# A two-block model kernel on one core: x loaded first and squared along rows, a stage's first block behind the evictions two blocks back, the residual ahead of the last modulation sum

## The chip, the cores and the metric

The kernel runs on one core of one Trainium2 chip. The core has TensorE (PE), VectorE (DVE), ScalarE (ACT), GpSimd (POOL), the sync engine (SP) that issues transfers, and 16 DMA engines that all queues share. The metric is the device time of one execution in microseconds (us). Lower is better.

## What is computed

The reference runs 512 tokens of width 1024 through two model blocks. The first has a gated linear recurrence (hgrn2), a sparse attention (nsa) and two swiglu layers, all with norms that are scaled and shifted by a modulation computed from a vector `c`. The second has a differential attention, a state-space layer (s5) and two squared-relu layers.

```
mods = einsum('bd,lde->lbe', silu(c), ada_w) + ada_b        # 4 x (1024 x 3072) products with one vector
shift, scale, gate = split(mods[2 * layer], 3)
h = rms_norm(x, gain) * (1 + scale) + shift                 # rms_norm: x * rsqrt(mean(x*x) + eps) * gain
x = x + gate * mixer(h)
... swiglu, then the second layer, then the second block
```

## The kernel before

Activations are kept transposed: `xT` is 128 partitions x 8 k-tiles x 512 tokens. Every weight product is done in blocks. A block is one weight tile of up to 128x2048 (1 MB), loaded into `raw` (a ring of two), split by ACT into a rounded part `whi` (`convert_hi`, L385) and by DVE into the rest `wlo` (`convert_lo`, L389), and multiplied by PE with the two parts `hh` and `hl` of the activations: three 512-column matmuls per 128x128 weight tile (L448, or L442 where the output is token-major; L426 and L430 in a stage that starts while its activations are still being made). PSUM has eight banks; a block with parity `par` writes banks `2 * par` and `2 * par + 1`, and banks 4 to 7 serve the sums.

The stages ("segments") stand in one list: h_q, h_f, h_v, h_g, h_out, ffn0_in0, ffn0_out0, ffn0_in1, ffn0_out1, n_kvc, n_ks, n_vs, n_kw, n_vw, n_q, n_out, then the same four ffn1 stages, d_q, d_k, d_v, d_out, the four mlp0 stages, s_glu and the four mlp1 stages. Each has `act` and `dve`, the number of its PSUM evictions per block that ACT and DVE do. The order of work on each engine is the order of the program; waits are on semaphores (`ev_a` and `ev_v` count evictions, `mm` counts finished units of PE, `w_lo` counts converted blocks). Before a block, `weight_products` waits for the evictions of the block two back, which used the same banks, counted by this stage's own rate. At a stage whose `(act, dve)` differs from the stage before, and that has no `need` of its own, `boundary` (L569) waits for all evictions of all stages before. There are nine such stages: h_v, ffn0_in1, n_vs, n_kw, n_vw, ffn1_in1, d_v, mlp0_in1 and mlp1_in1.

The start. SP issues the eight loads of `ada_first` (1 MB each, 128 rows of 8 KB, the first modulation matrix; a ring of six slots, so that the seventh and eighth load wait for `ada0_sum_v` and `ada0_used`, which say that DVE and PE have used a slot), then the weight loads `raw`. ACT issues five small constant loads, among them `ident` and `ones`, and then `xin` (x, 2 MB, rows of 4 KB). PE transposes the constants (L2582, waits for all five), multiplies the last four column groups of the first two modulation matrices with `cact` (L544), then transposes x into banks 0 to 3, 4 matmuls per k-tile (L2589). ACT squares each k-tile from PSUM into `sq` (L2160) and copies it to `xT` (L2161), and PE adds the squares over the partitions with a matmul by `ones` (L535, `first_square_sum`, 512 columns per k-tile) before it transposes on. Behind them stand the other six L544 groups and 12 matmuls (24 instructions) of `ada_sum` by `ones` (L556), which end the first modulation. DVE meanwhile multiplies and adds the eight `ada_first` tiles into `ada_sum` (L524, L527), then adds the bias (L2381), forms the gain (L2373), converts the first `wlo` and begins `apply`: for each k-tile xn = xT * gain * rstd (L2402), ACT makes `hh` (L2185), DVE makes `hl` (L2394). PE's first weight product is L426.

Later modulations are computed beside the stages: ACT loads (`ada_load`), DVE forms sums over k (`ada_sums`, L506 and L510, 8 instructions per block), PE adds them over the partitions (`ada_products`, L470) one block later, `ada_bias` adds the bias. In a stage that ends in a norm (`norm_after`: h_out, ffn0_out1, n_out and so on) DVE adds the residual (`residual`, L2439 or L2437), ACT squares it (L2202), PE sums the squares (`square_sums`, L2605), and at the end ACT makes `rstd` (L2177, L2178). Of these stages h_out alone also has modulation sums. In h_out's DVE code `ada_sums` stands ahead of the residual in every block, and in its PE code the last `ada_products` ahead of the last `square_sums`.

## Time and profile before

| | |
|---|---|
| median of 3 runs | 3031.37 us (3028.98 to 3031.47) |
| profiled execution | 3029.0 us |
| its span | 3027.3 us |
| PE busy | 2827.0 us, 93% of the span |
| DVE busy | 1654.6 us, 55% |
| ACT busy | 1063.9 us, 35% |
| mean granted TensorE clock | 0.968 |

The span is the time between the first and the last instruction that the profiler saw; the execution's own time is 1.7 us more. In a timeline row the columns are start in us, duration in us, engine, line, operation, output and inputs by the program's names, their sizes, and how many instructions were merged into the row; in brackets stands how long the engine had nothing to run before it and whose result ended that. Matmuls overlap, so a row's duration is longer than the distance to the next. ACTq and SPq rows are the issues of transfers, not their duration.

### The profile page before, as it was taken

The page shows a single profiled execution, that of the slowest core. Times are in us where ns is not written, and L with a number is a line of the kernel's source. Part 1 is how long each engine was busy: PE and PEld are TensorE (multiplying, and loading weights), DVE is VectorE, ACT ScalarE, POOL GpSimd, SP SyncE. Part 2 cuts the span into 40 slices and gives each one's busy share as a digit, 9 for nine tenths or more (in the row PEclk, how much of TensorE's full clock was granted, in tenths as well). Part 3 has the DMA queues.
Part 4 walks back from the last instruction along what each step waited for, and adds up shares of the span by engine and source line. Part 5 has one row for each costly group of instructions (what it writes and reads, how often), then busy time and mean ns, then how long its engine had stood idle before and what let it go on. Part 6 is the DMA issues. An engine that isn't in the chain of part 4 may idle for free.

```text
span 3027.3 us, 38551 instructions
## 1 busy us (share of the span) xinstructions
PE 2827.0 (93%) x14850; PEld 2262.7 (75%) x14850; DVE 1654.6 (55%) x2383; ACT 1063.9 (35%) x1577; POOL 75.2 (2%) x87
## 2 busy tenths in 40 slices
PE   6999999999988799999999998999999977999999
PEld 4898778888776556688787785777887756778787
DVE  4576566766453667433334557467677395353342
ACT  3312233222322367332223438433232534342231
POOL 2013000000000000000000100000000000000000
PEclk9999999999999799999999999999999988999999
DMA  5640356564424000232333330143444671223332
GB/s 212 195 140 1 112 153 191 163 182 144 154 86 128 1 1 1 56 83 81 107 84 111 114 100 13 42 100 103 141 153 153 230 125 57 84 83 98 97 97 70
DMA packets 400811, 321.14 MB, mean 106 GB/s; under 512 B 14409, under 2 KB 387233, under 8 KB 399649
## 3 DMA queue, kind: packets, MB, share of 16 engines
q1 hardware_dynamic: 324096, 237.19, 26.7%
q10 hardware_dynamic: 74496, 77.77, 7.9%
q0 software_dynamic: 2080, 4.26, 0.6%
q8 instruction: 96, 1.57, 0.2%
q14 instruction: 43, 0.34, 0.0%
HBM read 293.05 MB, written 19.86 MB: 103 GB/s over the span
## 4 chain that ended last, share of the span: by engine, by line
PE 64%; issue 22%; DVE 8%; ACT 2%; DMA 2%; POOL 1%; SPq 0%; ACTq 0%; DVEq 0%; POOLq 0%
PE ps L448 45%; PE ps L426 4%; PE ps L442 2%; PE ps L430 2%; DVE ada_acc L1749 1%; PE ps L873 1%; PE ps L903 1%; PE ps L885 1%; PE ps L1617 1%; PE ps L2605 1%; DVE h_area L1751 1%; DVE h_area L1753 1%; DMA xin<-in_x 1%; PE ps L1658 1%; POOL kT L1829 1%
## 5 line engine op out<-in xcount | busy, mean ns | idle before, releaser
L448 PE MATMUL ps<-hh,whi 128*128 128x512 f32 x1744 | 690.8, 396 | 5.1 <-DVE xT L2439 1.6
L448 PE MATMUL ps<-hh,wlo 128*128 128x512 f32 x1744 | 680.7, 390 | 0.0
L448 PE MATMUL ps<-hl,whi 128*128 128x512 f32 x1744 | 680.1, 390 | 0.0
L389 DVE TENSOR_TENSOR wlo<-raw,whi 128x2048 fp32r<-128x2048 f32 x198 | 453.9, 2292 | 359.7 <-ACT whi L385 359.7
L385 ACT ACTIVATE whi<-raw 128x2048 fp32r<-128x2048 f32 x198 | 377.3, 1906 | 380.8 <-PE ps L448 257.7
L448 PEld LDWEIGHTS ps<-hh,whi 128*128 128x128 f32 x1744 | 328.1, 188 | 79.3 <-issue 11.8
L448 PEld LDWEIGHTS ps<-hl,whi 128*128 128x128 f32 x1744 | 328.2, 188 | 70.3 <-issue 3.8
L448 PEld LDWEIGHTS ps<-hh,wlo 128*128 128x128 f32 x1744 | 327.9, 188 | 69.2
L448 PE MATMUL ps<-hid_h,whi 128*128 128x512 f32 x756 | 307.4, 407 | 0.0
L448 PE MATMUL ps<-hid_l,whi 128*128 128x512 f32 x756 | 298.9, 395 | 0.0
L448 PE MATMUL ps<-hid_h,wlo 128*128 128x512 f32 x756 | 298.8, 395 | 0.0
L448 PEld LDWEIGHTS ps<-hid_h,whi 128*128 128x128 f32 x756 | 142.2, 188 | 37.5 <-issue 4.3
L448 PEld LDWEIGHTS ps<-hid_l,whi 128*128 128x128 f32 x756 | 142.2, 188 | 37.4 <-issue 4.3
L448 PEld LDWEIGHTS ps<-hid_h,wlo 128*128 128x128 f32 x756 | 142.0, 188 | 34.6
L510 DVE SCALAR_TENSOR_TENSOR ada_ring<-ada_ring,cact 128x256 f32<-128x256 f32 (+1 forms) x336 | 151.8, 452 | 12.1
L2202 ACT ACTIVATE sq<-xT 128x512 f32 (+1 forms) x56 | 35.3, 632 | 291.5 <-DVE xT L2439 138.8
L2437 DVE TENSOR_TENSOR xT<-xT,ps 128x512 f32 (+1 forms) x40 | 27.4, 686 | 165.8 <-PE ps L448 144.7
L2263 ACT ACTIVATE hid_h<-hid_f 128x512 f32 (+1 forms) x44 | 27.8, 632 | 246.6 <-DVE hid_f L2485 246.6
L426 PE MATMUL ps<-hh,whi 128*128 128x512 f32 x176 | 78.0, 443 | 38.4 <-ACT hh L2185 38.4
L2325 ACT ACTIVATE act_t<-ps 128x512 f32<-128x512 f32 x64 | 38.0, 597 | 194.8 <-PE ps L448 185.9
L2539 DVE TENSOR_TENSOR hid_f<-act_t 128x512 f32<-128x512 f32 x64 | 43.4, 688 | 103.7 <-ACT act_t L2325 103.3
L2485 DVE TENSOR_TENSOR hid_f<-act_t,ps 128x512 f32<-128x512 f32 x44 | 30.2, 687 | 126.3 <-PE ps L448 121.3
(401 smaller groups left out, 4130.8 us busy)
## 6 DMA issues: line engine op xcount, KB each, us to landing
raw<-in_ffn_w_in SPq DMA_DIRECT2D x44, 1024.0 KB, 6.0
ada_ring<-in_ada_w ACTq DMA_DIRECT2D x82, 512.0 KB, 4.4
raw<-in_ffn_w_up SPq DMA_DIRECT2D x32, 1024.0 KB, 5.4
raw<-in_ffn_w_down SPq DMA_DIRECT2D x32, 1024.0 KB, 5.8
raw<-in_ffn_w_out SPq DMA_DIRECT2D x32, 704.0 KB, 4.6
raw<-in_hgrn_w_in SPq DMA_DIRECT2D x16, 1024.0 KB, 5.8
raw<-in_attn_w_qkv SPq DMA_DIRECT2D x12, 1024.0 KB, 5.1
s_area<-cp_dram SPq DMA_DIRECT2D x6, 2048.0 KB, 9.8
```

The source lines that it names most:

```text
L385: nc.scalar.activation(whi[:, par, :], raw[:, par, :], ACT.Copy).then_inc(w_hi, 1)
L389: nc.vector.tensor_tensor(wlo[:, par, :], raw[:, par, :], whi[:, par, :].bitcast(F32), ALU.subtract).then_inc(w_lo, 1)
L426: nc.tensor.matmul(ps[:, 2 * par + j, :], tile(w, kt, j), hi[:, kt, :], start=(kt == 0 and n == 0), stop=False)
L430: m = nc.tensor.matmul(ps[:, 2 * par + j, :], tile(wh, kt, j), lo[:, kt, :], start=False, stop=(kt == k - 1))
L442: m = nc.tensor.matmul(ps[:, bank, half * 256:half * 256 + 256], x[:, kt, t0:t0 + P], w[:, kt, :], start=(kt == 0 and n == 0), stop=(kt == ...
L448: m = nc.tensor.matmul(ps[:, bank, :], tile(w, kt, j), x[:, kt, :], start=(kt == 0 and n == 0), stop=(kt == k - 1 and n == 2))
L510: nc.vector.scalar_tensor_tensor(out=acc if last else w[:, 0, :], in0=w[:, kt, :], scalar=cact[:, kt:kt + 1], in1=w[:, 0, :], op0=ALU.mult ...
L873: m = nc.tensor.matmul(ps[:, S_BANK[w % 2] + i, 0:n], nqr[rows, p, t * P:(t + 1) * P], (k_sel, k_win)[br][rows, p // 2, 0:n], start=False, ...
L885: m = nc.tensor.transpose(ps[:, 2 + i, kt * P:(kt + 1) * P], pbuf[:, 2 * (w % P_SLOTS) + i, kt * P:(kt + 1) * P], ident[:, :])
L2202: nc.scalar.activation(sq[:, q:q + 1, :], xT[:, bass.ds(b * s.dve + j, 1), :], ACT.Square).then_inc(sq_rdy, 1)
L2325: nc.scalar.activation(act_t[:, j, :], ps[:, 2 * par + j, :], ACT.Relu).then_inc(ev_a, 1)
L2539: nc.vector.tensor_tensor(hid_f[:, j, :], act_t[:, j, :], act_t[:, j, :], ALU.mult).then_inc(hidf_rdy, 1)
```

## The change

The diff does three things.

1. The start. SP issues the load of x ahead of `ada_first`; ACT no longer issues it. PE transposes x right behind the constants, with the first L544 group (k-tile 0 of the modulation) after the fourth k-tile of x and the second after the eighth. ACT copies each k-tile of x to `xT`, and after every second one squares one 128-token tile of `xin` along its row (128x1024) with an accumulated output `x_ssq`, one column per tile. DVE, between its fourth and fifth modulation sum, spreads each column on a diagonal (`ident * x_ssq`, 128x128, four times), and PE multiplies these by `ones` (four matmuls of 128 columns in place of eight of 512). The 12 `ada_sum` matmuls run the scale columns (8 to 11) first, in bank 4, then the shift columns (0 to 7), in bank 6, and signal each part. DVE forms scale and gain after the first part, makes the first two xn, and only then waits for the second part, adds the shift and converts the first `wlo`.
2. Boundaries. Where `(act, dve)` changes and the stage has no `need`, the first block now waits as the stages with a `need` do, for the evictions up to the block two back, and `boundary` stands ahead of the second block.
3. h_out's last block. DVE does the residual first and `ada_sums` behind it; PE does the last `square_sums` ahead of the last `ada_products`.

```diff
--- before.py
+++ after.py
@@ -233,7 +233,7 @@
         ev_a = sem("ev_a")
         ev_v = sem("ev_v")
         const_a, const_in = sem("const_a_in"), sem("const_in")
-        x_in = sem("x_in")
+        x_in, x_sq = sem("x_in"), sem("x_squares")
         sq_rdy, ssq_rdy, rstd_rdy = sem("sq_rdy"), sem("ssq_rdy"), sem("rstd_rdy")
         xn_rdy, hh_rdy, hl_rdy = sem("xn_rdy"), sem("hh_rdy"), sem("hl_rdy")
         a_link, v_link, pool_set = sem("a_link"), sem("v_link"), sem("pool_set")
@@ -526,14 +526,26 @@
                     dve.wait_ge(ada0_sum_v, kt)
                     nc.vector.scalar_tensor_tensor(out=ada_sum[:, :], in0=w, scalar=c, in1=ada_sum[:, :],
                                                    op0=ALU.mult, op1=ALU.add).then_inc(ada0_sum_v, 1)
+                if kt == 3:
+                    first_square_spread(dve)
             dve.wait_ge(cols_ps, 2)
             link(nc.vector.tensor_copy(cols_b[:, 0:NROW_B], ps[:, 5, 0:NROW_B]))

-        def first_square_sum(pe, kt):
-
-            pe.wait_ge(sq_rdy, kt + 1)
-            nc.tensor.matmul(ps[:, 7, :], ones[:, :], sq[:, kt % 2, :], start=(kt == 0),
-                             stop=(kt == KT - 1)).then_inc(ssq_rdy, 1)
+        x_ssq = gains_a[:, 4, 0:TT]
+
+        def first_square_spread(dve):
+
+            for t in range(TT):
+                dve.wait_ge(x_sq, t + 1)
+                nc.vector.tensor_scalar(rstd[:, t * P:(t + 1) * P], ident[:, :], x_ssq[:, t:t + 1], None, ALU.mult
+                                        ).then_inc(sq_rdy, 2)
+
+        def first_square_sums(pe):
+
+            for t in range(TT):
+                pe.wait_ge(sq_rdy, 2 * t + 2)
+                nc.tensor.matmul(ps[:, 7, t * P:(t + 1) * P], ones[:, :], rstd[:, t * P:(t + 1) * P], start=True, stop=True,
+                                 skip_group_check=True).then_inc(ssq_rdy, 2)

         def ada_first_pe(pe, k0, k1):

@@ -552,10 +564,11 @@
             if k1 < FIRST:
                 return
             pe.wait_ge(ada0_sum_v, FIRST)
-            for j in range(NV):
-                m = nc.tensor.matmul(ps[:, 4, j:j + 1], ada_sum[:, j * P:j * P + P], ones[:, 0:1],
-                                     start=False, stop=True, skip_group_check=True)
-            m.then_inc(ada0_used, 1)
+            for bank, part in ((4, range(KT, NV)), (6, range(KT))):
+                for j in part:
+                    m = nc.tensor.matmul(ps[:, bank, j:j + 1], ada_sum[:, j * P:j * P + P], ones[:, 0:1],
+                                         start=(j == 0), stop=True, skip_group_check=True)
+                m.then_inc(ada0_used, 1)

         def ada_bias(dve, s):

@@ -2053,6 +2066,7 @@
         @block.sync
         def _(sp):

+            sp.dma_start(xin[:, :, :], a["x"][0].rearrange("(t p) d -> p t d", p=P)).then_inc(x_in, 16)
             for kt in range(FIRST):
                 if kt >= 6:
                     sp.wait_ge(ada0_sum_v, kt - 5)
@@ -2149,16 +2163,19 @@
             act.dma_start(vec_a[0:96, :], a["ada_b"].rearrange("l (c n) -> (l c) n", n=P)).then_inc(const_a, 16)
             act.dma_start(vec_a[96:112, :], a["kv_ada_b"].rearrange("(c n) -> c n", n=P)).then_inc(const_a, 16)
             act.dma_start(ones[:, :], a["k_ones"]).then_inc(const_a, 16)
-            act.dma_start(xin[:, :, :], a["x"][0].rearrange("(t p) d -> p t d", p=P)).then_inc(x_in, 16)
             act.wait_ge(cols_rdy, 1)
             nc.scalar.activation(cact[:, :], cols_a[:, ROWS["c"]:ROWS["c"] + 8], ACT.Silu).then_inc(cact_rdy, 1)
             log_table()
+            act.wait_ge(x_in, 16)
             for kt in range(KT):
                 act.wait_ge(mm, kt + 1)
-                if kt >= 2:
-                    act.wait_ge(ssq_rdy, kt - 1)
-                nc.scalar.activation(sq[:, kt % 2, :], ps[:, kt % 4, :], ACT.Square).then_inc(sq_rdy, 1)
                 nc.scalar.activation(xT[:, kt, :], ps[:, kt % 4, :], ACT.Copy).then_inc(ev_v, 1)
+                if kt % 2:
+                    t = kt // 2
+                    if t >= 2:
+                        act.wait_ge(x_sq, t - 1)
+                    nc.scalar.activation((sq, xn)[t % 2][:, :, :].rearrange("p s n -> p (s n)"), xin[:, t, :], ACT.Square,
+                                         accum_out=x_ssq[:, t:t + 1]).then_inc(x_sq, 1)
             act.wait_ge(pool_set, 2)

             def norm(m, x_count):
@@ -2378,9 +2395,12 @@
             ada_first_dve(dve, link)
             dve.wait_ge(ada0_used, FIRST + 1)
             dve.wait_ge(cols_rdy, 1)
-            link(nc.vector.tensor_tensor(mods[:, 0:16], ps[:, 4, 0:16], cols_a[:, 0:16], ALU.add))
-            modulated_gain(0, ROWS["norm_mix"], 8).then_inc(mods_rdy, 1)
-            if upto >= 2:
+            link(nc.vector.tensor_tensor(mods[:, 8:16], ps[:, 4, 8:16], cols_a[:, 8:16], ALU.add))
+            link(modulated_gain(0, ROWS["norm_mix"], 8))
+
+            def first_shift():
+                dve.wait_ge(ada0_used, FIRST + 2)
+                nc.vector.tensor_tensor(mods[:, 0:8], ps[:, 6, 0:8], cols_a[:, 0:8], ALU.add).then_inc(mods_rdy, 1)
                 convert_lo(dve, segs[0], 0, 0, 0)

             def apply(j, m, gain, shift, h_free):
@@ -2402,14 +2422,20 @@
                     nc.vector.scalar_tensor_tensor(out=xn[:, k % 2, :], in0=xT[:, kt, :],
                                                    scalar=gain[:, kt:kt + 1], in1=rstd[:, :],
                                                    op0=ALU.mult, op1=ALU.mult).then_inc(xn_rdy, 1)
+                    if j == 0 and kt == 1:
+                        first_shift()
                     if kt:
                         low(k - 1)
                 low(KT * j + KT - 1)

             def linear(s, evac):
                 def body(b, par, more):
-                    ada_sums(dve, s, b, par)
+                    late = s.name in norm_after and isinstance(b, int) and b == s.n - 1
+                    if not late:
+                        ada_sums(dve, s, b, par)
                     evac(b, par)
+                    if late:
+                        ada_sums(dve, s, b, par)
                     if s.name in D0:
                         d_hook_dve(dve, link, D0[s.name] + b)
                     if more:
@@ -2451,7 +2477,6 @@
                 return evac

             if upto >= 2:
-                dve.wait_ge(mods_rdy, 1)
                 apply(0, 0, *mod_cols(0), FIRST_UNITS)
                 convert_lo(dve, segs[0], 0, 1, 1)
                 linear(seg["h_q"], none)
@@ -2580,18 +2605,18 @@
         def _(pe):
             pe.wait_ge(const_a, 16 * 5)
             nc.tensor.transpose(ps[:, 6, 0:NROW_A], vec_a[0:NROW_A, :], ident[0:NROW_A, 0:NROW_A]).then_inc(cols_ps, 1)
-            ada_first_pe(pe, 0, 2)
             pe.wait_ge(x_in, 16)
             for kt in range(KT):
                 if kt >= 4:
                     pe.wait_ge(ev_v, kt - 3)
                 for t in range(TT):
-                    m = nc.tensor.transpose(ps[:, kt % 4, t * P:(t + 1) * P], xin[:, t, kt * P:(kt + 1) * P],
-                                            ident[:, :])
+                    m = nc.tensor.transpose(ps[:, kt % 4, t * P:(t + 1) * P],
+                                            xin[:, t, kt * P:(kt + 1) * P], ident[:, :])
                 m.then_inc(mm, 1)
-                if kt:
-                    first_square_sum(pe, kt - 1)
-            first_square_sum(pe, KT - 1)
+                if kt % 4 == 3:
+                    ada_first_pe(pe, kt // 4, kt // 4 + 1)
+            ada_first_pe(pe, 2, 4)
+            first_square_sums(pe)

             def square_sums(s, m, b, par):

@@ -2618,9 +2643,7 @@

                 prev = segs[segs.index(s) - 1] if s.g0 else None
                 change = prev is not None and (prev.act, prev.dve) != (s.act, s.dve)
-                if change and need is None:
-                    boundary(pe, s)
-                elif change:
+                if change:
                     if s.ea0 - prev.act > 0:
                         pe.wait_ge(ev_a, s.ea0 - prev.act)
                     pe.wait_ge(ev_v, s.ev0 - prev.dve)
@@ -2630,7 +2653,7 @@

                 def body(b, par, more):
                     first = isinstance(b, int) and b == 0
-                    if change and need is not None and isinstance(b, int) and b == 1:
+                    if change and isinstance(b, int) and b == 1:
                         boundary(pe, s)
                     weight_products(pe, s, b, par, hi, lo, token_major, need if first else None)
                     if s.ada and not first:
@@ -2644,12 +2667,12 @@
                     unrolled(s, body, D0, lambda db: d_hook_pe(pe, db))
                 else:
                     each_block(pe, s, body, need is not None or m is not None or s.ada is not None)
-                ada_products(pe, s, s.n - 1, (s.g0 + s.n - 1) % 2)
                 if m is not None:
                     square_sums(s, m, s.n - 1, (s.g0 + s.n - 1) % 2)
+                ada_products(pe, s, s.n - 1, (s.g0 + s.n - 1) % 2)

             if upto >= 2:
-                ada_first_pe(pe, 2, FIRST)
+                ada_first_pe(pe, 4, FIRST)
                 linear(seg["h_q"], need=(hl_rdy, 0))
                 linear(seg["h_f"])
                 linear(seg["h_v"], token_major=True)
```

## Rows read from the trace of the kernel before

**Rows 1.** The page's first part: busy time, share of the span, instructions.
```profile
PE 2827.0 (93%) x14850; PEld 2262.7 (75%) x14850; DVE 1654.6 (55%) x2383; ACT 1063.9 (35%) x1577; POOL 75.2 (2%) x87
```

**Rows 2.** Timeline, issues of the first transfers on the ACT and SP queues.
```profile
0.82 19.15 SPq L2060 DMA_DIRECT2D ada_first<-in_ada_w  x8
...
3.54 0.56 ACTq L2152 DMA_DIRECT2D xin<-in_x  x1
...
20.02 102.32 SPq L2075 DMA_DIRECT2D raw<-in_hgrn_w_in  x9
```

**Rows 3.** Stretches: length, busy PE PEld DVE ACT POOL; clock, DMA share, GB/s.
```profile
24.00:28.00 4.00, 0.00 (x0) 0.00 (x0) 3.79 (x3) 0.00 (x0) 0.00 (x0) 1.00 1.01 417
...
47.50:53.00 5.50, 5.21 (x25) 5.12 (x25) 0.17 (x1) 0.00 (x0) 0.00 (x0) 0.50 0.00 0
```

**Rows 4.** Timeline of PE from 14 to 58 us.
```profile
14.92 0.46 PE L2582 MATMUL ps<-ident,vec_a 120*128 120x120 f32 x1 [14.92 <-DMA ones<-in_k_ones]
...
29.29 1.97 PE L2589 MATMUL ps<-ident,xin 128*128 128x128 f32 x8 [9.72 <-DMA xin<-in_x]
...
43.83 3.76 PE L544 MATMUL ps<-cact,ada_first 128*128 128x1 f32 x32
47.45 5.26 PE L556 MATMUL ps<-ones,ada_sum 128*128 128x1 f32 x24
57.00 0.77 PE L426 MATMUL ps<-hh,whi 128*128 128x512 f32 x1 [4.29 <-ACT hh L2185]
```

**Rows 5.** Timeline of DVE up to 57 us.
```profile
29.71 1.82 DVE L527 SCALAR_TENSOR_TENSOR ada_sum<-ada_first,cact,ada_sum 128x1536 f32<-128x1536 f32 x1 [1.18 <-DMA ada_first<-in_ada_w]
...
52.80 0.17 DVE L2381 TENSOR_TENSOR mods<-ps,cols_a 128x16 f32<-128x16 f32 x1 [8.49 <-PE ps L556]
...
55.30 1.41 DVE L2402 SCALAR_TENSOR_TENSOR xn<-xT,gains_a,rstd 128x512 f32<-128x512 f32 x2
```

**Rows 6.** Timeline of ACT up to 46 us.
```profile
15.96 1.28 ACT L642 ACT_TABLE_LOAD   x1
...
30.93 0.59 ACT L2161 ACTIVATE xT<-ps 128x512 f32<-128x512 f32 x1
...
43.50 1.89 ACT L385 ACTIVATE whi<-raw 128x2048 fp32r<-128x2048 f32 x1
```

**Rows 7.** Timeline of PE where a stage's first block waits at a boundary.
```profile
151.37 0.39 PE L442 MATMUL ps<-whi,hh 128*128 128x256 f32 x1 [0.49 <-ACT kT L2222]
...
610.01 0.47 PE L448 MATMUL ps<-hh,whi 128*128 128x512 f32 x1 [0.70 <-issue]
...
846.56 0.39 PE L442 MATMUL ps<-whi,hh 128*128 128x256 f32 x1 [0.69 <-ACT nsa_area L2222]
...
859.16 0.47 PE L448 MATMUL ps<-hh,whi 128*128 128x512 f32 x1 [0.83 <-issue]
...
1464.72 0.39 PE L448 MATMUL ps<-hid_l,whi 128*128 128x512 f32 x1
1464.96 0.40 PE L448 MATMUL ps<-hid_h,wlo 128*128 128x512 f32 x1
1466.90 0.47 PE L448 MATMUL ps<-hh,whi 128*128 128x512 f32 x1 [1.55 <-DVE xT L2439]
...
2840.59 0.49 PE L448 MATMUL ps<-hh,whi 128*128 128x512 f32 x1 [1.32 <-DVE xT L2437]
```

**Rows 8.** Timeline of DVE, last block of h_out and the norm behind it.
```profile
406.44 0.35 DVE L506 TENSOR_SCALAR ada_ring<-ada_ring,cact 128x256 f32<-128x256 f32 x1 [0.82 <-DMA ada_ring<-in_kv_ada_w]
...
410.42 1.40 DVE L2439 SCALAR_TENSOR_TENSOR xT<-ps,mods,xT 128x512 f32<-128x512 f32 x2
414.50 2.29 DVE L389 TENSOR_TENSOR wlo<-raw,whi 128x2048 fp32r<-128x2048 f32 x1 [2.68 <-ACT whi L385]
...
416.98 1.42 DVE L2402 SCALAR_TENSOR_TENSOR xn<-xT,gains_a,rstd 128x512 f32<-128x512 f32 x2
```

**Rows 9.** Timeline of PE beside it, behind h_out's last weight product.
```profile
408.84 1.96 PE L2605 MATMUL ps<-sq,ones 128*128 128x512 f32 x4
```

## The prediction, made before the changed kernel was run

> **What bounds the kernel now.** I read four views in this order. The page first: PE is busy for 93% of the span [rows 1], so time is gained only where PE stands still or runs slowly, and work that leaves DVE or ACT is worth nothing by itself. Then the timeline of PE, for its gaps. The longest stretch without weight products is the start: the first one begins at 57.00 [rows 4]. Then the stretches and the issues of transfers, for what holds the start. Up to some 29 us it is the DMA engines: they are full (share 1.01, 417 GB/s) [rows 3]. x (2 MB) is issued by ACT at 3.54 behind the constants, while SP has given eight 1 MB loads since 0.82 [rows 2]; PE gets x only at 29.29 [rows 4], 25.7 us after the issue, and DVE gets its last modulation tile at 29.71 [rows 5]: both end together, because they share the engines. From there the start is a chain on PE, one thing behind the other: x's transposes with the square sums, six column groups of the modulation, 24 instructions on `ada_sum`, then on DVE bias, gain, `wlo` and xn, then 57.00 [rows 4, 5]. Last I read the waits at the places that the other two parts touch [rows 7 to 9].
>
> **Part 1, the start.** The bytes in front of the last modulation tile are the same (x 2 MB, `ada_first` 8 MB, constants), and the engines are full, so this tile lands at 29.7 as before; what is new is that x is long done by then. I take the new chain step by step.
>
> *Constants and x.* The trace doesn't show a queue with x first. Before, the constants' last row was in at 14.92 [rows 4] beside 8 KB rows of `ada_first`; x has 4 KB rows, so if the queues take turns by rows, a small row waits half as long. From the issue at about 3.5 the 11.4 us become some 6, plus what x doesn't cover: I take 11.5. Ends: 8.5 (nothing but x's 2 MB at 417 GB/s, 5 us, after 3.5) and 14.9 (no change). x itself then lands by 10 and is not last.
>
> The Trainium skill, DMA: Bandwidth & Descriptors, "Queues, rings and completion order", says that each engine goes round the queues that have work, a packet at a time; by that, x behind ACT's queue had every second turn against rows of twice its size. The trace agrees: 25.7 us for 2 MB. The same page ("Issuing engines are not separate DMA queues") speaks against the change: which engine issues changes nothing of the bandwidth. So by it too only the order matters, and the last tile stays at 29.7.
>
> *PE and ACT.* At 14.92 + 0.46 to 29.29 PE ran cold: 8 transposes (two k-tiles) took 1.97 [rows 4], 1.0 per k-tile. So from 12.0: four k-tiles 4.0, one L544 group 1.75 (8 instructions, each 0.219 as in L556: 5.26 / 24), four k-tiles 4.0: 21.8. ACT needs, per pair of k-tiles, two copies at a pitch of about 0.5 (0.59 long) and one 1024-wide square, about 1.0, between the 0.59 for 512 and the 1.89 for 2048 [rows 6]; it keeps pace from the end of its table load (1.28, 15.96 before [rows 6]), and its last square ends about 1.6 behind PE: 23.4. DVE's four spreads (128x128, nearest row 0.17, taken 0.2 each, last one only behind the last square) end at 24.0.
>
> *DVE.* Four sums at 1.82 and their waits, 7.6: 31.6. By the last tile alone it is 29.71 + 1.82 = 31.5 [rows 5]. So both limits meet; I take 31.8. The square sums on PE (8 short instructions) and `rstd` (two 0.7 activations) lie in the wait for tiles 5 to 7, and the conversion of `whi` (1.89 [rows 6]) as well: its tile comes two to three us behind the last modulation tile (1 MB at 417 GB/s is 2.5), at about 33, done at 35.
>
> *The tail.* The clock: at 47.5 to 53 the granted clock was 0.50 (1.2 GHz) while PE did nothing but one-column matmuls [rows 3], at 0.219 each; ahead of that 32 of them took 3.76, 0.118 each [rows 4], behind dense work. In the changed kernel PE mostly waits for tiles before them: I take 0.219. Scale columns, 8 instructions: 1.75, to 33.6. Bias and gain: 52.80 to the next conversion was 0.3 before, 0.4 now with one more link: 34.0. First two xn, 1.41 [rows 5]: 35.4. Shift columns, 16 instructions, 3.5: 37.1; they end later than xn, so they are the path. Shift add 0.2, `wlo` 2.29 [rows 8]: 39.6. First weight product at 39.7 instead of 57.00. The first block's own rhythm is the same as before (two xn were ahead of it then too), and later loads are set off by its progress, so the whole rest moves with it. **Gain 17.3.** Bounds: with the constants at 14.9 PE and DVE are 3.4 later, 43.1, gain 13.9; with the sums at 0.118 the scale columns end at 32.4, xn at 34.3, shift at 34.5, start at 36.9, gain 20.1.
>
> The Trainium skill, TensorE: Matmul & The Clock Gate, "Part 1: The HAM clock gate", says that half clock is the resting state and activity lifts it. The granted clock of the stretch agrees (0.50 through busy one-column work); by the page the tail is at half clock in the changed kernel, which is the value that I took.
>
> **Part 2, nine boundaries.** Here PE waits for the eviction of the block that it has just ended. What is lost is the idle time of the row plus the overlap that a following matmul would have had: 0.40 long at a pitch of 0.24 [rows 7], so 0.16 more (0.09 behind one-column matmuls). h_v 0.49 + 0.09 = 0.58; ffn0_in1 0.70 + 0.14 = 0.84; n_vs 0.69 + 0.16 = 0.85, and n_vw has the same row; n_kw 0.83 + 0.16 = 0.99; ffn1_in1 1.55 + 0.16 = 1.71; mlp1_in1 1.32 + 0.16 = 1.48 [rows 7]. d_v and mlp0_in1 have other PE work at the boundary, which hides the eviction already: 0 to 0.2, taken 0.1 for both. **Sum 7.4.** The new block writes the other pair of banks, its weights are converted a block ahead, and the new wait is for evictions a whole block (8 to 11 us) old, so nothing comes in place of the old one. The evictions themselves stay on ACT and DVE with nothing moved. Upper end 7.5; lower end 3, if half is taken by what the trace calls issue (two of the rows) [rows 7].
>
> **Part 3, h_out.** The last tile of modulation weights came only at 406.4, so `ada_sums` ran to 410.42, and both residual steps behind it, to 411.8 [rows 8]; PE had ended the block by 408.84 [rows 9]. Now the second residual runs at 408.7 to 409.4, 2.4 us earlier. Its square by ACT, PE's sums and `rstd` follow and come 1.5 us earlier (PE is held by the sums of block 2, 408.84 + 1.96 [rows 9]). But DVE then has its 3.98 of `ada_sums` between residual and conversion: 413.4, `wlo` 2.29 to 415.6, bias and gain 0.4, xn at 416.1 instead of 416.98 [rows 8]. **Gain 0.9**: the path moves from `rstd` to DVE. Ends: +1.5 (only `rstd` counts) and -2.4 (if the residual didn't get earlier but the 3.98 stood behind it).
>
> **Sum.** 17.3 + 7.4 + 0.9 = 25.6. Against the profiled execution of 3029.0 this gives 3003.4; that execution lies 2.4 below the median of 3031.37. For the median of such runs I add it back: **3005.8**.
>
> **The rivals.**
> - *A, the constants come no earlier.* For it: they are many small rows on ACT's queue, as before. Against: x's rows are half as long. PE's first transposes slip to 15.4, and DVE, in order, holds sums 5 to 8 behind the spreads. Gain 13.9 + 8.3 = 22.2: 3009.2.
> - *B, TensorE at full clock in the tail.* For it: x's transposes and the square sums run close ahead. Against: the gaps between tiles. Gain 28.4: 3003.0.
> - *C, the boundary waits go but PE doesn't start earlier*, because part of those gaps is the sequencer's. Gain 17.3 + 3 + 0.9 = 21.2: 3010.2.
> - *D, slower.* The place is the first stages behind the start: PE's clock was 0.50 at 47.5 to 53 [rows 3], and a weight product costs twice its pitch at that level (0.24 becomes about 0.43 to 0.48). If the calmer start left the clock at half for longer than before, each us of it would cost 0.5 against the full clock. It would decide from 51 us more of half clock on (25.6 x 2), some five blocks of h_q and h_f; through eight blocks (about 90 us of work at full clock) it would cost 90 and end near 3095. Against it: dense products followed the same idle state before, too.
>
> **Chances.** Forecast 0.50, A 0.15, B 0.15, C 0.14, D 0.03, and 0.03 for a result within 0.2% (6 us, about what a measurement of this kernel can tell from no change), if x or the slots of `ada_first` are so late that the start loses nearly all of its gain. Forecast, A, B and C are all faster by more than 0.2%. The forecast's own range is 3002 to 3009; with A to C and the scatter of the medians it is 2999 to 3014. Faster 0.94, same 0.03, slower 0.03.
>
> **What would show it.** Right: constants at 10 to 13, x's first transpose directly behind; DVE's eighth sum still at 29 to 30; first L426 at 37 to 43; no idle in front of the first matmul at the seven boundaries; in h_out the residual ahead of L506 and xn about 1 us earlier after the block. Wrong: the eighth sum well behind 32 (then the ring or the spreads hold it), the idle at a boundary under another releaser, or a later stage with more idle than before that takes the gain back.

## The result, and the profile after

The changed kernel takes 3004.28 us (median of 4 runs, 3001.33 to 3005.76) against 3031.42 us (4 runs, 3028.98 to 3037.92): ratio 0.9906, 95% interval 0.9891 to 0.9922, so 27.1 us less. The profiled execution took 3001.33 us, its span is 2999.6 (before 3029.0 and 3027.3). The forecast was 3005.8.

The page's first part after the change. Columns are as in [rows 1]:
```profile
PE 2817.7 (94%) x14842; PEld 2258.0 (75%) x14842; DVE 1655.1 (55%) x2388; ACT 1064.1 (35%) x1577; POOL 76.0 (3%) x87
```
PE's busy time fell by only 9.3 us; the rest of the 27.7 us of span is idle time that went.

The issues of the first transfers on SP and ACT's queue (timeline, start and length), answering [rows 2]:
```profile
0.82 0.43 SPq L2069 DMA_DIRECT2D xin<-in_x  x1
1.31 3.67 SPq L2074 DMA_DIRECT2D ada_first<-in_ada_w  x6
...
3.02 0.65 ACTq L2165 DMA_DIRECT2D ones<-in_k_ones  x1
```
The stretches, columns as in [rows 3]:
```profile
0.00:4.00 4.00, 0.00 (x0) 0.00 (x0) 0.00 (x0) 0.31 (x1) 2.94 (x12) 1.00 0.42 117
...
24.00:28.00 4.00, 3.62 (x17) 3.65 (x18) 3.79 (x4) 1.32 (x2) 0.00 (x0) 0.50 1.01 420
28.00:32.00 4.00, 2.93 (x14) 2.84 (x15) 2.69 (x2) 0.00 (x0) 0.00 (x0) 0.50 1.04 362
```
PE from 13 to 41 us (start, length, idle before), answering [rows 4]:
```profile
13.35 0.46 PE L2607 MATMUL ps<-ident,vec_a 120*128 120x120 f32 x1 [13.35 <-DMA ones<-in_k_ones]
13.61 3.33 PE L2613 MATMUL ps<-ident,xin 128*128 128x128 f32 x16
...
17.58 1.94 PE L2613 MATMUL ps<-ident,xin 128*128 128x128 f32 x16
...
31.14 1.87 PE L556 MATMUL ps<-cact,ada_first 128*128 128x1 f32 x8 [1.07 <-DMA ada_first<-in_ada_w]
32.99 5.28 PE L569 MATMUL ps<-ones,ada_sum 128*128 128x1 f32 x24
40.73 0.79 PE L426 MATMUL ps<-hh,whi 128*128 128x512 f32 x1 [2.46 <-DVE wlo L389]
```
DVE beside it, answering [rows 5]:
```profile
23.95 0.29 DVE L540 TENSOR_SCALAR rstd<-ident,gains_a 128x128 f32<-128x128 f32 x1 [1.33 <-ACT xn L2177]
...
31.12 1.82 DVE L527 SCALAR_TENSOR_TENSOR ada_sum<-ada_first,cact,ada_sum 128x1536 f32<-128x1536 f32 x1 [1.31 <-DMA ada_first<-in_ada_w]
...
34.95 0.17 DVE L2398 TENSOR_TENSOR mods<-ps,cols_a 128x8 f32<-128x8 f32 x1 [1.82 <-issue]
...
35.35 1.41 DVE L2422 SCALAR_TENSOR_TENSOR xn<-xT,gains_a,rstd 128x512 f32<-128x512 f32 x2
38.31 0.17 DVE L2403 TENSOR_TENSOR mods<-ps,cols_a 128x8 f32<-128x8 f32 x1 [1.54 <-PE ps L569]
38.39 2.28 DVE L389 TENSOR_TENSOR wlo<-raw,whi 128x2048 fp32r<-128x2048 f32 x1
```
ACT's squares and the first `whi`, answering [rows 6]:
```profile
16.66 1.06 ACT L2177 ACTIVATE sq<-xin 128x1024 f32<-128x1024 f32 x1
...
23.59 0.26 ACT L2177 ACTIVATION_READ_ACCUMULATOR xn<-xin 128x1 f32 x1
...
33.95 1.91 ACT L385 ACTIVATE whi<-raw 128x2048 fp32r<-128x2048 f32 x1 [7.35 <-DMA raw<-in_hgrn_w_in]
```
Nothing of x is late any more: its transposes, with one modulation group between, end at 19.5, the squares at 23.85. What ends last is a transfer, the eighth modulation tile at 31.1, and behind it a chain of PE and DVE alone: scale columns, gain, two xn, shift columns, `wlo`. The first weight product is at 40.73 instead of 57.00 [rows 4]: **16.3 us**.

The boundaries of [rows 7], PE's timeline again: h_v, ffn0_in1, ffn1_in1 and mlp1_in1, with one row ahead of each of the first three:
```profile
133.61 0.95 PE L470 MATMUL ps<-ones,ada_acc 128*128 128x1 f32 x8
134.42 0.36 PE L442 MATMUL ps<-whi,hh 128*128 128x256 f32 x1
...
591.29 0.25 PE L470 MATMUL ps<-ones,ada_acc 128*128 128x1 f32 x1
591.40 0.48 PE L448 MATMUL ps<-hh,whi 128*128 128x512 f32 x1
...
1441.85 0.39 PE L448 MATMUL ps<-hid_h,wlo 128*128 128x512 f32 x1
1442.09 0.39 PE L448 MATMUL ps<-hh,whi 128*128 128x512 f32 x1
...
2813.06 0.39 PE L448 MATMUL ps<-hh,whi 128*128 128x512 f32 x1
```
No row carries an idle bracket now, and at 1441.85 the next product follows at the usual 0.24. The last block of h_out, DVE and then PE, answering [rows 8, 9]:
```profile
391.77 0.75 DVE L2465 SCALAR_TENSOR_TENSOR xT<-ps,mods,xT 128x512 f32<-128x512 f32 x1 [2.36 <-PE ps L448]
392.44 0.34 DVE L506 TENSOR_SCALAR ada_ring<-ada_ring,cact 128x256 f32<-128x256 f32 x1
...
396.51 2.29 DVE L389 TENSOR_TENSOR wlo<-raw,whi 128x2048 fp32r<-128x2048 f32 x1
...
398.98 1.42 DVE L2422 SCALAR_TENSOR_TENSOR xn<-xT,gains_a,rstd 128x512 f32<-128x512 f32 x2
```
```profile
391.94 3.92 PE L2630 MATMUL ps<-sq,ones 128*128 128x512 f32 x8
396.55 0.60 PE L470 MATMUL ps<-ones,ada_acc 128*128 128x1 f32 x4 [0.70 <-DVE ada_acc L510]
400.64 0.76 PE L426 MATMUL ps<-hh,whi 128*128 128x512 f32 x1 [3.48 <-ACT hh L2202]
```
The residual is now ahead of L506, as written.

**Where the time came from.** I compared the start of each stage in the two traces; the lead over the kernel before grows in steps (us):

| place | predicted | measured |
|---|---|---|
| first weight product | 17.3 | 16.3 |
| h_v, ffn0_in1, n_kw, n_vw | 0.58, 0.84, 0.99, 0.85 | 0.68, 0.86, 1.09, 0.94 |
| n_vs | 0.85 | 1.77, about 0.9 of it a half-clock stretch at the start of n_kvc, 2.6 us long instead of 4.7 |
| ffn1_in1, mlp1_in1 | 1.71, 1.48 | 1.71, 1.48 |
| h_out to ffn0_in0 | 0.9 | 1.1 |
| d_v and mlp0_in1 together | 0.1 | 0.14, read a block behind |
| end of the span | 25.6 | 27.7 |

With 0.85 for n_vs the three parts make 16.3 + 7.6 + 1.1 = 25.0, and 0.14 more come at d_v and mlp0_in1. What is left of the 27.7 stands at places that the change doesn't touch, and is a sum of gains and losses; experiment e9 is about it. Two of its terms aren't the clock's. In mlp0_in0 the kernel before waits 0.86 at 2014.08 for the load `ada_ring<-in_ssm_c_im`, and the changed one doesn't. And at the first product of n_q, the stage behind n_vw, PE waits for ACT's `hh`, 5.89 before and 6.29 after:
```profile
866.58 0.77 PE L426 MATMUL ps<-hh,whi 128*128 128x512 f32 x1 [6.29 <-ACT hh L2202]
```
There the lead falls from 22.49 to 22.09. So 0.4 of what part 2 gained at the three nsa boundaries ahead of it is given back. From the last product of n_vw to the first of n_q it is 6.57 in every profile with part 2, and 6.17 in the four without (before, e1, e3, e4).

### The profile page after: what moved, and what is told of

Its sections match the earlier page's. It is cut to its first block, busy times and chain, and to the rows that moved or that the text cites. A ratio compares the mean times of both kernels' runs of the same rounds, so it can differ in the third digit from the quotient of the medians.

```text
span 2999.6 us, 38549 instructions
## 1 busy us (share of the span) xinstructions
PE 2817.7 (94%) x14842; PEld 2258.0 (75%) x14842; DVE 1655.1 (55%) x2388; ACT 1064.1 (35%) x1577; POOL 76.0 (3%) x87
## 3 DMA queue, kind: packets, MB, share of 16 engines
q1 hardware_dynamic: 324624, 239.29, 27.1%
## 4 chain that ended last, share of the span: by engine, by line
PE 66%; issue 22%; DVE 7%; ACT 2%; DMA 1%; POOL 1%; SPq 0%; ACTq 0%; DVEq 0%; POOLq 0%
PE ps L448 47%; PE ps L426 4%; PE ps L442 2%; PE ps L430 2%; DVE ada_acc L1762 1%; PE ps L886 1%; PE ps L916 1%; PE ps L898 1%; PE ps L2630 1%; PE ps L1630 1%; DVE h_area L1766 1%; DVE h_area L1764 1%; PE ps L1671 1%; POOL kT L1842 1%; PE ps L2035 1%
## 5 line engine op out<-in xcount | busy, mean ns | idle before, releaser
L2510 DVE TENSOR_TENSOR hid_f<-act_t,ps 128x512 f32<-128x512 f32 x44 | 30.2, 686 | 124.5 <-PE ps L448 120.2
```

Source lines behind the costliest of these rows:

```text
L2510: nc.vector.tensor_tensor(hid_f[:, par, :], act_t[:, par, :], ps[:, 2 * par + 1, :], ALU.mult).then_inc(ev_v, 1)
```

## The experiments

Ratios are to the kernel before, run beside each on the same chip. "Lead" is the kernel's lead over it at a place of the trace.

**e1, part 1 alone.** The changed kernel with parts 2 and 3 put back:
```diff
-                if change:
+                if change and need is None:
+                    boundary(pe, s)
+                elif change:
```


> Part 1 of the change alone (the start). Theory P (the parts add up, each worth what its own place in the trace shows): the first weight product starts at 40.7 us as in the changed kernel, the seven boundary waits and h_out are as before, and the time is 16.3 us below before (ratio 0.9946). Rival Q (the start shifts what later transfers meet, and part of the 27 us comes from stages with no edit): the time falls by 19 us or more.

Measured: 3017.57 us (5 runs, 3015.03 to 3018.05) against 3031.96; ratio 0.9952 (0.9938 to 0.9965). The lead is 16.15 at the first product and 13.96 at the end. The interval, 10.6 to 18.8 us less, holds theory P's 16.3 and not rival Q's 19. So part 1 carries over nearly whole; 1.5 of the lost 2.2 go in one stage, and e2 shows how.

**e2, part 2 alone**, on the kernel before:
```diff
-                    if change and need is not None and isinstance(b, int) and b == 1:
+                    if change and isinstance(b, int) and b == 1:
```


> Part 2 alone (the boundaries). Theory P: the idle in front of the first product of h_v, ffn0_in1, n_vs, n_kw, n_vw, ffn1_in1 and mlp1_in1 is gone, 7.4 us in sum; ratio 0.9976. Rival R (part of those gaps is the sequencer's own time): the first products still start 0.3 to 0.7 us behind the last product of the stage before, 3 to 4 us in sum, ratio 0.9988. The first weight product stays at 57.0.

Measured: 3024.02 us (11 runs); ratio 0.9978 (0.9969 to 0.9987). Steps of the lead: h_v 0.60, ffn0_in1 0.85, n_kw 1.09, n_vw 0.94, ffn1_in1 1.71, mlp1_in1 1.48. They come without the other parts, and to 0.1 us as large as with them. The lead at the end is 6.4 in the profile. Of what is missing 1.5 is lost in the recurrence's stage and 0.4 ahead of n_q; the rest is gains and losses elsewhere. The stretch just behind PE's 2.3 us wait there, of e2 and then, 0.65 later, of the kernel before (columns as in [rows 3]):
```profile
209.35:213.35 4.00, 4.00 (x24) 4.00 (x23) 3.70 (x4) 0.00 (x0) 0.52 (x1) 0.57 0.00 0
```
```profile
210.00:214.00 4.00, 4.00 (x38) 4.00 (x37) 4.00 (x5) 0.00 (x0) 0.51 (x1) 1.00 0.00 0
```
The same work, PE busy for all 4 us in both, but 24 matmuls at a clock of 0.57 instead of 38 at 1.00.

**e3, part 3 alone**, on the kernel before: `ada_sums` moved behind `evac` in the last block of h_out, and `ada_products` behind `square_sums`:
```diff
                     evac(b, par)
+                    if late:
+                        ada_sums(dve, s, b, par)
```


> Part 3 alone (h_out's last block). Theory P: from the last product of h_out to the first one of ffn0_in0 the distance falls by 1.0 us (18.0 - 16.9 = 1.1 in the changed kernel), with DVE's conversion of wlo as the last thing ahead of xn, rstd done 1.5 earlier. Rival S: it is a clock effect of the sums on PE and the distance stays. The whole time can't tell 1 us; the trace does.

Measured, one run: 3029.4 us; the lead is -0.32 ahead of h_out's end and 1.10 larger behind it, as theory P has it, though `rstd` comes 1.1 earlier against the block and not 1.5. By total time one run can't tell that; the trace can. What 1.10 is measured from varies, though: from the start of h_out's last product to ffn0_in0's first it is 10.40 before, 10.36 in e2, 9.57 in e1 and 11.25 in e4, where the last square sums ran at half clock (3.53 instead of 1.99); with part 3 it is 9.30 in every profile but e8's (9.36).

**e4, only x's place in the queues**, all else as before:
```diff
+            sp.dma_start(xin[:, :, :], a["x"][0].rearrange("(t p) d -> p t d", p=P)).then_inc(x_in, 16)
             for kt in range(FIRST):
```


> Before, with one edit: SP issues x ahead of ada_first, ACT does not. The squares stay per k-tile with 512-column sums on PE, and all 24 ada_sum instructions stand ahead of bias and gain. Theory X (the order of the loads alone takes PE's work off the chain behind x): x lands at about 9, its transposes and square sums end at about 28, the last modulation tile is summed at 33.0, L556 ends at 38.3, wlo at 41, first weight product at 42.8: 14.2 us earlier than before, and 2.1 later than the changed kernel. Rival Y (the squares along rows carry a good part): first weight product at 46 or later.

Measured: 3021.33 us (8 runs, 3017.12 to 3026.47); ratio 0.9963 (0.9952 to 0.9973). First product at 48.8, a lead of 8.2: half of part 1. PE's timeline of e4, three rows:
```profile
17.95 1.95 PE L2589 MATMUL ps<-ident,xin 128*128 128x128 f32 x8
...
29.84 1.98 PE L535 MATMUL ps<-sq,ones 128*128 128x512 f32 x4
31.65 1.84 PE L544 MATMUL ps<-cact,ada_first 128*128 128x1 f32 x16
...
39.27 5.26 PE L556 MATMUL ps<-ones,ada_sum 128*128 128x1 f32 x24
```
The 512-wide square sums of the old form and the transposes keep PE until 31.65; the modulation groups stand behind them, so PE is the late one, not the last tile. The rival was right and my expectation wrong: an early x is worth its full price only together with the rest of part 1. DVE's last modulation sum in e4:
```profile
30.02 1.82 DVE L527 SCALAR_TENSOR_TENSOR ada_sum<-ada_first,cact,ada_sum 128x1536 f32<-128x1536 f32 x1 [0.76 <-DMA ada_first<-in_ada_w]
```
So with x first the last tile was in at 30.0 here, not at 31.1.

**e5, the rest of part 1 with x at its old place**, behind the constants on ACT's queue:
```diff
-            sp.dma_start(xin[:, :, :], a["x"][0].rearrange("(t p) d -> p t d", p=P)).then_inc(x_in, 16)
@@ at the end of the constants
+            act.dma_start(xin[:, :, :], a["x"][0].rearrange("(t p) d -> p t d", p=P)).then_inc(x_in, 16)
```


> The changed kernel with the load of x given back to ACT's queue, behind the constants; everything else changed (row squares, split sums, boundaries, h_out). Theory X2 (the new order on PE and DVE needs x early: the seventh and eighth ada_first load wait for ada0_used, which PE now signals only behind four and eight transposed k-tiles, and DVE holds its last four sums behind the spreads): x lands at 29, the seventh load is issued at about 35 and the eighth at about 39, the eighth sum ends at 46, first weight product at 54, so of the start's 16.3 only about 3 are left; time 14 below before (ratio 0.9954). Rival Z (x's place in the queues is worth only what its transposes are): first product at 47 or earlier.

Measured: 3016.9 us (4 runs) against 3032.62; ratio 0.9945 (0.9931 to 0.996). x was in at 24.7, 4.6 earlier than before at the same place of the queue, and the first product at 51.4: a lead of 5.6, at a place ahead of parts 2 and 3. My expectation was 2.6 too late (54), and rival Z (47) is out. The wait for a free slot worked as I had it, but it held the seventh load back to 29.98, so that only six tiles stood beside x, and x came earlier than the 29 that I took. So of the 16.3, x alone brings 8.2 (e4), and everything else of part 1 (the squares, the order on PE, the split of the columns) 5.6; together 2.5 more than the sum of both, since each uncovers the other.

**e6, the modulation columns not split** (DVE waits for all 24 before bias and gain):
```diff
-            dve.wait_ge(ada0_used, FIRST + 1)
+            dve.wait_ge(ada0_used, FIRST + 2)
```


> The changed kernel, but DVE forms scale and gain only after the shift columns too. Theory: xn comes behind the 16 shift instructions instead of beside them; first weight product at 42.6 instead of 40.7, so the split is worth 1.9 of the start's 16.3. Rival: DVE's chain is bound by the conversion of wlo or by the raw tile (landed 33.9), and the start stays at 40.7.

Measured, one run: 3007.83 us, first product at 42.63. The split is worth 1.9 us, as expected. It puts gain and the two xn under the 16 shift columns, though those are now in front of `wlo`.

**e7, the first `wlo` before the wait for the shift columns.** In the changed kernel DVE idles 1.54 at 38.31 while `whi` has been ready since 35.86, and `wlo` (2.28) comes only then:
```diff
-                    if j == 0 and kt == 1:
+                    if j == 0 and kt == 0:
+                        convert_lo(dve, segs[0], 0, 0, 0)
                         first_shift()
```


> The changed kernel with DVE's first conversion of wlo and the shift add moved between the first and the second xn, into the 1.5 us in which DVE waits for the shift columns. Theory: the conversion runs 36.1 to 38.4, hh at 38.6 to 39.3, first weight product at 39.3, 1.4 earlier. Rival: the second xn and the first hl then come later and the first block runs at DVE's pace, so that its end comes no earlier (block 2 still at 54.3).

Measured: 3002.86 us (4 runs, 2999.79 to 3004.76); ratio 0.9905 (0.9891 to 0.9919). PE's timeline of e7:
```profile
39.45 0.77 PE L426 MATMUL ps<-hh,whi 128*128 128x512 f32 x1 [1.10 <-ACT hh L2202]
...
53.08 0.50 PE L448 MATMUL ps<-hh,whi 128*128 128x512 f32 x1 [0.58 <-DVE wlo L389]
```
1.3 us earlier than the changed kernel at the first product, 1.2 at the second block (54.32), so the rival is out. It is ahead of both kernels in the trace; its time and the changed kernel's (3004.28) can't be told apart.

**e8 and e11, PE kept at full clock.** The 24 instructions L569 take 5.28 at a clock of 0.50. e8 puts a 512-column matmul whose result nobody reads ahead of six of the modulation groups and of L569; e11 puts it ahead of four groups only:
```diff
+                if kt >= 2:
+                    keep_warm(pe)
```


> The changed kernel with seven more 128x512 matmuls of ones by x into the idle bank 3, one ahead of each modulation tile that PE waits for from the third on and one ahead of the ada_sum matmuls; their results are not used. Theory B (the one-column matmuls behind an idle PE run at half clock, 0.220 each): with the clock kept at 1.00 the 24 sum instructions take 2.9 instead of 5.3, wlo ends at 38.2, first product at 38.4, and the first block, which spent 2.5 us at half clock, ends another 1 us earlier: h_q's second block at about 51. Rival B2 (one-column matmuls run at half pace whatever stands around them, or the extra work only delays them): sum instructions stay at 0.22 and the first product comes at 41 to 43.

> The changed kernel with only four unused 128x512 matmuls, ahead of modulation tiles 5 to 8, none ahead of the ada_sum matmuls. With seven of them the clock stayed at 1.00 and the sums took 2.73 instead of 5.28, but they began at 35.7 instead of 33.0. Theory M (four keep the clock and leave PE no backlog): sums start at 33.0 to 33.3 and take 2.7, first product at 38.4. Rival N (four are too few or still too much): the sums take 5.3, or start at 34 and later, and the first product comes at 40 or later.

Measured: e8 3013.46 us (6 runs, 3005.93 to 3024.66), ratio 0.994 (0.9923 to 0.9956); e11 3012.55 us (4 runs), ratio 0.9933 (0.9916 to 0.9951); both slower than the changed kernel by their medians (e11's four runs all lie above e9's five, the changed kernel on the same chip). PE's timeline, e8 first, then e11:
```profile
34.72 1.10 PE L553 MATMUL ps<-xin,ones 128*128 128x512 f32 x2
35.66 2.73 PE L577 MATMUL ps<-ones,ada_sum 128*128 128x1 f32 x24
40.85 0.79 PE L426 MATMUL ps<-hh,whi 128*128 128x512 f32 x1 [2.46 <-DVE wlo L389]
```
```profile
25.89 1.89 PE L553 MATMUL ps<-xin,ones 128*128 128x512 f32 x2
...
39.38 5.26 PE L576 MATMUL ps<-ones,ada_sum 128*128 128x1 f32 x24
47.09 0.79 PE L426 MATMUL ps<-hh,whi 128*128 128x512 f32 x1 [2.46 <-DVE wlo L389]
```
In e8 the clock held and L577 took 2.73 instead of 5.28, but it began 2.7 later, since the extra matmuls of 0.95 each had queued PE up: the first product gained nothing. The fall only came later, at about 39 us, while PE waited for `wlo`. That doesn't explain e8's longer time: its second block starts at 54.44 against 54.32, so e8 loses its 7 to 9 us behind the start, in stages without an edit. Its profile ends 11.2 behind the first one of the changed kernel, and 7.5 of that stand at the two places that e9 shows below; why its runs are longer on the whole stays open. In e11 the clock fell as the first extra matmul began (25.9; 1.89 for two rows that take 1.10 in e8), and the next ones took 1.85 each: 6.4 us lost at the first product, and 6.0 in time against the changed kernel on the same chip (3006.51, e9). So theory B was right on the clock and wrong on the first product, and e11 went as rival N had it.

e8 shows one thing more. Its loads stand in the changed kernel's order, yet DVE's last four sums run without a wait:
```profile
24.46 7.58 DVE L527 SCALAR_TENSOR_TENSOR ada_sum<-ada_first,cact,ada_sum 128x1536 f32<-128x1536 f32 x4
```
The last starts at 30.2, so the last tile was in by then, against 31.1 in the changed kernel.

**e9, the changed kernel again**, unaltered, on another chip.

> The changed kernel once more, not one line different. Theory G (what a stage gains or loses beyond its edit, 1 to 2 us here and up to 5.6 in the state-space stage, is how long TensorE's granted clock stays at half after a wait, which differs from one execution to the next): the half-clock starts of ffn0_in0, n_kvc, n_q, ffn1_in0, d_q and mlp0_in0 last between 2.5 and 5.5 us and not the same as in the first profile (4.6, 2.6, 2.6, 2.6, 4.6, 2.5), while the start (40.7) and the seven boundaries come out the same within 0.2. Rival H (these lengths belong to the code's timing): all of them come out as before within 0.2.

Measured: 3006.51 us (5 runs, 3005.03 to 3009.19) against 3033.53; ratio 0.9912 (0.9897 to 0.9927), 27.0 us less. First product at 40.83, the boundary steps as before to 0.1. Yet this profile's span is 3007.5, 7.9 longer than the first one's with the same code. By place, 1.5 of it come in the recurrence, where the clock was at half for 3.4 us behind PE's 2.3 us wait as in e2, and 5.7 in the state-space stage. That stage from its last weight product ahead to the first behind, the changed kernel's first profile and then e9's (columns as in [rows 3]):
```profile
2338.77:2530.54 191.77, 144.21 (x1606) 123.16 (x1604) 116.91 (x227) 85.68 (x141) 0.31 (x1) 0.88 0.55 149
```
```profile
2340.40:2537.91 197.51, 149.18 (x1607) 127.88 (x1605) 116.88 (x227) 86.32 (x141) 0.31 (x1) 0.85 0.53 144
```
DVE is busy for the same 116.9, PE for 5.0 more, at a lower mean clock. These two make some 7.3 of the 7.9; elsewhere gains and losses nearly cancel. Weight products also run at half clock (pitch 0.43 instead of 0.23) where a stage begins. Adding up the distances of 0.38 to 0.52 between them gives 39 us before, 35 in the first profile after, 42 in e9's. A us of them costs 1 - 0.23 / 0.43 = 0.46, so 4 us less explain 1.7 of what the first profile had beyond its parts, by this estimate. So theory G holds and rival H is out: the start and the boundaries repeat, the half-clock stretches don't.

The recurrence's 1.5 was lost in eight of the thirteen profiles (e1, e2, e4, e5, e6, e8, e9, e11) and not in the others, and the state-space stage was 5.4 to 5.7 longer than before in three (e5, e8, e9), 2.3 longer in two (e1, e6). The changed kernel's own two profiles differ at both places, so neither loss belongs to the code alone.

**e10, x behind the first modulation tile**, on top of e7:
```diff
+                if kt == 0:
+                    sp.dma_start(xin[:, :, :], a["x"][0].rearrange("(t p) d -> p t d", p=P)).then_inc(x_in, 16)
```


> The kernel with the early wlo conversion (first product at 39.45) and x as SP's second load, behind the first modulation tile. Theory K (with 4 KB rows of x first the engines fill late, 117 instead of 155 GB/s up to 4 us, and that is why the last tile lands at 31.1 and not at 29.7): the last sum starts at 30.2 to 30.7 and the first product at 38.6 to 39.0. Rival L (the constants land later behind 8 KB rows, 14 or more, and PE and DVE reach the spreads later than they have slack for): last sum at 31.5 or later, first product at 39.8 or later.

Measured: 3003.73 us (4 runs); ratio 0.9908 (0.989 to 0.9926). PE's timeline and the first stretch of e10:
```profile
11.69 0.46 PE L2608 MATMUL ps<-ident,vec_a 120*128 120x120 f32 x1 [11.69 <-DMA ones<-in_k_ones]
12.33 3.68 PE L2614 MATMUL ps<-ident,xin 128*128 128x128 f32 x16 [0.17 <-DMA xin<-in_x]
...
31.04 1.87 PE L556 MATMUL ps<-cact,ada_first 128*128 128x1 f32 x8 [2.02 <-DMA ada_first<-in_ada_w]
...
39.28 0.76 PE L426 MATMUL ps<-hh,whi 128*128 128x512 f32 x1 [1.11 <-ACT hh L2203]
```
```profile
0.00:4.00 4.00, 0.00 (x0) 0.00 (x0) 0.00 (x0) 0.18 (x1) 2.94 (x12) 1.00 0.49 155
```
I had held the slower first 4 us (117 GB/s against 155) to be why the last tile comes at 31.1 instead of 29.7. e10 gives the 155 back and the tile still comes at 31.0, so that theory falls. Its rival, that small rows wait longer behind large ones, falls too: the constants came at 11.69, earlier than behind x. As to the first product theory K (38.6 to 39.0) and rival L (39.8) both missed 39.28; it is 0.17 ahead of e7's. What sets 31.1 stays open. It isn't x's place alone: with x first the last tile is in at 31.1 to 31.2 in the changed kernel, e1, e6, e7, e9 and e11, but at 30.0 in e4 and by 30.2 in e8, and e8 and e9 issued it at the same time (23.15 and 23.17). No run tried other sizes of the transfers.

## Why the prediction was right, and where it missed

- *What bounds the start*: right. PE's and DVE's first rows waited for x [rows 4, 5] only because x and `ada_first` shared the engines; with x first the start went to the last modulation tile and the chain behind it. e4 and e5 show that both x's place and the rest of part 1 are needed.
- *Constants*: predicted 11.5, measured 13.35, inside the bounds 8.5 and 14.9. Taking x's row size as the measure was wrong, as e10 shows. It cost nothing: PE had been up to date again at 24.38, where it waits for a spread of 23.95 (predicted 24.0), and DVE at 31.12, idle for 1.31. That the spread hit 24.0 is luck: the constants were 1.85 late, and the prediction had PE take 9.8 for the eight k-tiles and one group, at half clock throughout; they took 5.9, since the second four k-tiles ran at full clock (1.94 for 16 instructions, 3.33 for the first 16). ACT's pace of 2.0 per pair set the end. Rival A had its delay cost 3.4; the slack in front of the last tile was larger than it assumed. The prediction also calls x's 25.7 us agreement with an even turn of the two queues, which says too much: 25.7 us at some 417 GB/s are 10.7 MB, of which x is a fifth, while every second turn at half the size would be a third.
- *The last tile*: this is the step that missed. "This tile lands at 29.7 as before" came out as 31.1; its sum ended at 32.94 instead of 31.8. That is all of the start's miss (16.3 for 17.3). Equal bytes ahead of a transfer on full engines gave landings of 29.7 before, 31.1 after, 30.0 in e4 and by 30.2 in e8. So the failed term is a landing time taken from one profile as if it were exact; the cause of the spread stays open.
- *The tail*: from the sum's end to the first product predicted 39.7 - 31.8 = 7.9, measured 40.73 - 32.94 = 7.8, each link within 0.2. The value that carries it is 0.219 for a one-column matmul, 5.28 / 24 measured. The Trainium skill, TensorE: Matmul & The Clock Gate, "Part 1: The HAM clock gate", puts an idle engine at half clock. The fall in the changed kernel doesn't speak against it: it comes between 23 and 24 us, where PE idles for 1.10 ahead of 24.38. But the clock then stayed at 0.50 at 24 to 28 although PE was busy for 3.62 of 4 us, and in the kernel before it fell with no idle at all: the mean is 1.00 at 44 to 46, 0.80 at 46 to 48 and 0.50 behind, while PE had been busy since 29.29, with one-column matmuls, but for one transpose, since 41.99. So the prediction's reading that the trace agrees with a clock lifted by activity holds for dense matmuls, not for these; the value taken was right. Rival B (full clock) is out, and e8 shows that even getting it doesn't pay. B's price was also a slip of 0.3: 31.8 plus eight at 0.118 is 32.7, not 32.4.
- *The boundaries*: right in every one, 7.6 with 0.85 for n_vs against 7.3 for the seven. The idle plus 0.16 for the lost overlap is the right price at the boundary: ffn1_in1 and mlp1_in1 came out at it to 0.01. "Nothing comes in place of the old one" missed the 0.4 that is given back ahead of n_q. Rival C, in which the idle named "issue" stays, is out: ffn0_in1 and n_kw, the two such rows, gave 0.86 and 1.09.
- *h_out*: 1.1 against 0.9. xn starts at 398.98, 18.0 earlier than 416.98 with 16.9 gained before. The path is where it was put, on DVE, but not by `ada_sums` alone: `whi` ends at 396.47 and `ada_sums` at 396.50, so `wlo` waits equally for both.
- *The rest*: the places sum to 25.0 (25.6 predicted), and medians fell 27.1 and 27.0. Both intervals (23.6 to 33.0 and 22.1 to 31.2 us, from the ratios) hold either number, so the 2 us between them aren't shown to be real. Rival D, slower through a longer half clock, is out as to its size: among the weight products the lengths changed by 4 us between the kernels and by 7 between two executions of one. That the span fell by 27.7, more than the parts, is luck of the first profile; e9's fell by 19.8.

## What to carry to other kernels

When DMA engines are full, what counts is which tile PE needs first and whether the work on it can be finished under the later tiles; moving the transfer alone (8.2 us) or changing the work alone (5.6) was worth less than both together (16.3). The landing of the last tile is itself only known to some 1.5 us from one profile. A wait at a stage boundary is priced by its idle bracket plus the overlap that the next matmul loses (0.40 - 0.24 here), and lifting it by one block of double buffering returned all of it at the next product; look then at the next stage's first wait, which took 0.4 back here. For gains under a few us, compare where stages begin in the traces: two executions of the same code differed by 7.9 us in span, some 7.3 of it in two stages.

## What the hardware showed that I had not expected

- One-column matmuls didn't hold the clock: it fell at 46 to 48 us in the kernel before, on a PE that had not idled since 29.29, and was 0.50 at 24 to 28 in the changed one with PE busy for 3.62 of 4. With 512-column matmuls between them (e8) the granted clock was at full and 24 of them took 2.73.
- A half-clock stretch at a stage's start lasted from 2.5 us to some 6 (e4, 48.8 to 54.9), and differed at the same stage between executions of one code (at the first stage 2.5, and 4.7 in e9). The same 2.3 us wait in the recurrence was followed by full clock in five profiles and by 3.4 us of half clock in eight, for 1.5 us.
- Small constants issued at 0.8 to 3.7 us landed at 14.92 [rows 4], 13.35 and 11.69 according to the order on the other queues: `ada_first` alone, x then `ada_first`, one tile then x (e10). The row size of the neighbours doesn't explain this order.
- The clock column was wrong at the very start: it says 1.00 at 12 to 16 us of the changed kernel, where 16 transposes took 3.33, and 1.00 again for the next 16, which took 1.94. There the durations are the better reading.
